# Adding the last block's rows of a routed expert layer from SBUF with one-hot products instead of through memory

## The reference, cut to what matters

```python
vl = rmsnorm(hl, norm2_g[i]) * (1.0 + sc2) + sh2
hl = hl + g2 * moe_ffn(vl, ...)          # i = 0, then Hyena, then i = 1
...
def moe_ffn(xt, ...):
    # best group of 4, two best experts of its 8, weights g_w * e_w
    ...                                   # rows sorted by expert into blocks
    gate, up = split(xblk @ w13[e], 2)
    yb = (silu(gate) * up) @ w2[e]
    return segment_sum(yb * row_w[:, None], row_tok)
...
return rmsnorm(hl, final_g)
```

## Time and profile before

| What | Value |
|---|---|
| Runs | 2173.26 us median (2172.42 to 2173.95) |
| The profiled execution's own time | 2173.9 us |
| Its span | 2172.2 us, 21060 instructions |
| Mean granted TensorE clock | 0.977 of full |
| PE busy | 2006.0 us (92%) |
| DVE, ACT, POOL busy | 798.1, 399.3, 237.8 us (37%, 18%, 11%) |
| DMA | 582.54 MB, mean 268 GB/s |
| Copy of the hidden values (line 856), once per block | 73 times |
| Scatters (line 478) | 73 |

### The profile page before, as it was taken

One profiled execution on the slowest core, in us unless ns is written; L12 is line 12 of the kernel. 1 busy time (PEld: TensorE's weight loads), 2 busy tenths in 40 slices (PEclk: granted clock), 3 DMA queues, 4 the chain that ended last, 5 costly groups with the idle time before them and its releaser, 6 DMA issues. The chain is left out here.

```text
span 2172.2 us, 21060 instructions
## 1 busy us (share of the span) xinstructions
PE 2006.0 (92%) x7704; PEld 894.5 (41%) x7704; DVE 798.1 (37%) x1599; ACT 399.3 (18%) x813; POOL 237.8 (11%) x517
## 2 busy tenths in 40 slices
PE   5999999999999979999999988999997999888883
PEld 2555444454444544433333334444554344333331
DVE  3777321245323252225223524474735122111113
ACT  2111213223200121132113212110002111111111
POOL 1000000000000012212222210000000222222221
PEclk9999999999999979999999999999998999999997
DMA  9899432231114289999999973120255999999995
GB/s 369 300 372 355 167 124 90 90 109 61 58 59 148 88 357 407 392 411 420 414 422 400 422 277 119 62 91 26 103 246 205 392 421 421 423 422 422 422 422 218
DMA packets 117567, 582.54 MB, mean 268 GB/s; under 512 B 25599, under 2 KB 43255, under 8 KB 78028
## 3 DMA queue, kind: packets, MB, share of 16 engines
q1 hardware_dynamic: 90892, 538.32, 62.0%
q10 hardware_dynamic: 14560, 26.12, 3.4%
q0 software_dynamic: 12000, 16.62, 2.1%
HBM read 565.62 MB, written 38.12 MB: 278 GB/s over the span
## 5 line engine op out<-in xcount | busy, mean ns | idle before, releaser
L628 PE MATMUL bank<-w,xT 128*64 128x512 f32 x1856 | 414.0, 593 | 17.4 <-DMA w<-in_moe_w 16.3
L648 PE MATMUL bank<-w,hT 128*64 128x512 f32 x1168 | 273.3, 610 | 31.8 <-DMA w<-in_moe_w 23.7
L628 PEld LDWEIGHTS bank<-w,xT 128*64 128x64 f32 x1856 | 145.6, 137 | 271.9 <-issue 251.1
L856 DVE COPY hT<-bank 128x256 f32<-128x256 f32 x73 | 31.0, 424 | 451.8 <-PE bank L636 451.8
L1290 PE MATMUL bank<-uhi,wnh 128*128 128x512 f32 x384 | 168.4, 593 | 0.9 <-ACT uhi L1047 0.9
L648 PEld LDWEIGHTS bank<-w,hT 128*64 128x64 f32 x1168 | 87.0, 139 | 179.1 <-issue 151.7
L540 ACT ACTIVATE oh<-bank 128x256 f32<-128x256 f32 x73 | 28.0, 384 | 698.3 <-PE bank L628 698.3
L1688 PE MATMUL bank<-uT,wo 128*128 128x512 f32 x256 | 133.1, 602 | 3.0 <-DMA wo<-in_m_in_w 3.0
L861 DVE TENSOR_TENSOR ohs<-bank,g2h 128x512 f32<-128x512 f32 x73 | 50.5, 692 | 209.2 <-PE bank L648 209.2
L628 PE MATMUL bank<-w13x,xT 128*64 128x512 f32 x480 | 109.1, 594 | 4.0 <-DMA w13x<-in_moe_w 4.0
L1290 PEld LDWEIGHTS bank<-uhi,wnh 128*128 128x128 f32 x384 | 71.8, 190 | 86.9 <-issue 85.8
(11 more groups left out here) (453 smaller groups left out, 2237.2 us busy)
## 6 DMA issues: line engine op xcount, KB each, us to landing
w<-in_moe_w SPq DMA_DIRECT2D x172, 2048.0 KB, 19.4
adab<-in_ada_w SPq DMA_DIRECT2D x24, 2048.0 KB, 11.5
w13x<-in_moe_w SPq DMA_DIRECT2D x23, 2048.0 KB, 16.7
wnh<-in_h_in_w SPq DMA_DIRECT2D x12, 1024.0 KB, 5.2
wo<-in_m_in_w SPq DMA_DIRECT2D x4, 2048.0 KB, 17.8
wo<-in_m_in_w ACTq DMA_DIRECT2D x4, 2048.0 KB, 21.6
ow<-in_m_out_w SPq DMA_DIRECT2D x8, 1024.0 KB, 7.5
d_xm<-xmb ACTq DMA_DIRECT2D x16, 385.5 KB, 7.5
```

The lines of the kernel that those rows point to most:

```text
L628: ins = t_.matmul(b[n * C:(n + 1) * C, :].rearrange("c (g f) -> c g f", g=2), xT[:, k, half * C:(half + 1) * C], w13s[i][:, k, n], start=( ...
L648: ins = t_.matmul(b_y[m * C:(m + 1) * C, :], hT[:, k, half * C:(half + 1) * C], w2[:, u, kk, m * 512:(m + 1) * 512], start=(kk == 0), stop ...
```

## The change

The rows of block 36 (the last of the 36 steps) are no longer scattered. From the routing DVE builds, at step 3, a matrix over tokens and rows that holds the routing weight where a token's choice lies in block 36 (`last_hot`); at step 4 PE turns it (`last_turn`) and DVE copies it to `lastT`. In `drain`, PE multiplies it with `yb` (`last_rows`: eight products of 64 rows by 512 columns, into eight banks), and DVE adds the eight banks to `hl`. PE's first `extra` waits for all eight adds. Because some rows of `d_y` are now never written, `blank_results` fills each `d_y` with zeros beforehand: in `c4` for layer 0, in the Hyena stage for layer 1.

`load_results` moves from the start of the next stage to the end of SP's work in the expert stage, behind a new semaphore `end` that POOL raises when its scatters have landed. It now has fixed buffers in the weight rings. The router tables of layer 1 are loaded from ACT's queue late in the Hyena stage. `one32` becomes a slice of `ones`; `ohb` shares memory with `lastT`, and the new one-hot tiles lie in `dfe`. Cut to its core:

```diff
+LAST_TURN = 4
...
+        results = [[put(f"yg{l}{i}", [P, 4, D], W13 + pos * HALF) for i, pos in enumerate(((3, 4), (0, 1))[l])] for l in range(2)]
+        yg = [[tile_[:, 2 * i:2 * i + 2, :] for tile_ in results[l] for i in range(2)] for l in range(2)]
...
+        def blank_results(sp, l, blank, s_):
+            sp.dma_start(d_y[l].rearrange("(p a) (b n) -> p (a b) n", p=P, b=2), blank[:].to_broadcast([P, 16, 512])).then_inc(s_, 16)
...
+                LASTB = (0, 1, 2, 3, 6, 7, 4, 5)
+                def scattered(n):
+                    return len([b for b in range(1, n + 1) if b % 2 == n % 2 and b != NS])
...
@@ expert stage, SP
                     steps(sp, main, lambda: None, extra)
-                    if l == 0:
-                        load_route_tables(sp, 1)
+                    sp.wait_ge(S["end"], 1)
+                    load_results(sp, l)
@@ expert stage, POOL
                     def drain():
-                        scatter(NS)
                         for s in range(NS, NS + NB):
...
                     for u in range(2):
-                        pool.wait_ge(s_yst[u], (NS + u) // 2 * 16)
+                        pool.wait_ge(s_yst[u], 16 * scattered(NS - 1 + (NS - 1 + u) % 2))
+                    g.tensor_tensor(pad[:, 2 * NB:], ident[:, 0:2], ident[:, 0:2], ALU.add).then_inc(S["end"], 1)
@@ expert stage, PE, in main(s), before product2(s)
+                        if s == LAST_TURN:
+                            last_turn()
...
+                    def last_turn():
+                        pe.wait_ge(S["oh"], 1)
+                        for t in range(TL):
+                            ins = t_.transpose(bank[7][:, t * P:(t + 1) * P], ohl[:, t, :], ident[:])
+                        ins.then_inc(S["ohT"], 1)
+                    def last_rows():
+                        pe.wait_ge(S["ya"], NS)
+                        pe.wait_ge(S["xTa"], NS)
+                        pe.wait_ge(S["xTv"], NS)
+                        for t in range(TL):
+                            for m in range(2):
+                                rows = slice(m * C, (m + 1) * C)
+                                t_.matmul(bank[LASTB[2 * t + m]][:], lastT[rows, t * P:(t + 1) * P], yb[NS % 2][rows, :], start=True, stop=True).then_inc(S["lr"], 1)
                     def drain():
                         h_transposes(NS)
                         product2(NS)
+                        last_rows()
                     def extra(s):
+                        pe.wait_ge(S["la"], 2 * TL)
                         first(s)
@@ expert stage, DVE, at the end of main(b)
+                        if b == LAST_TURN - 1:
+                            last_hot()
+                        if b == LAST_TURN:
+                            dve.wait_ge(S["ohT"], 1)
+                            own(v.tensor_copy(lastT[:], bank[7][:]))
+                    def last_hot():
+                        own(v.tensor_scalar(sbf[:], sbf[:], float(NS - 1), 2.0 * P, ALU.not_equal, ALU.mult))
+                        own(v.tensor_tensor(spf[:], spf[:], sbf[:], ALU.add))
+                        own(v.tensor_tensor(eq, i64[:].to_broadcast([P, 2 * TL, P]), spf[:].to_broadcast([P, 2 * TL, P]), ALU.is_equal))
+                        pairs = eq.rearrange("p (t k) n -> p t k n", k=2)
+                        own(v.tensor_tensor(pairs, pairs, wts[:].rearrange("p k (t o) -> p t k o", o=1).to_broadcast([P, TL, 2, P]), ALU.mult))
+                        v.tensor_tensor(ohl, pairs[:, :, 0], pairs[:, :, 1], ALU.add).then_inc(S["oh"], 1)
...
                     def drain():
                         h_turned(NS)
                         y_out(NS)
+                        for i in range(2 * TL):
+                            rows = hl[:, i // 2, i % 2 * 512:(i % 2 + 1) * 512]
+                            dve.wait_ge(S["lr"], i + 1)
+                            v.tensor_tensor(rows, rows, bank[LASTB[i]][:], ALU.add).then_inc(S["la"], 1)
@@ Hyena stage, SP
-                    load_results(sp, 0, yg, s_yg)
...
                         load_slab(sp, wn, s_wn, q)
+                        if q == 4:
+                            sp.wait_ge(S["pad"], 3)
+                            blank_results(sp, 1, blank, S["yz"])
@@ Hyena stage, ACT, before the squares for the router
+                    load_route_tables(act, 1)
@@ c4, SP
                 load_w13(sp, 0, 2)
+                sp.wait_ge(s_blank, 1)
+                blank_results(sp, 0, blank, s_yz)
                 sp.wait_ge(s_o4, TL)
@@ final stage, SP
-                load_results(sp, 1, yg, s_yg)
```

More of the change, by code:

```diff
@@ L183, in build @@
         s_rt = [sem(f"s_rt{l}") for l in range(2)]
+        s_yg = [[sem(f"s_yg{k}{t}") for t in range(TL)] for k in range(2)]
+        results = [[put(f"yg{l}{i}", [P, 4, D], W13 + pos * HALF) for i, pos in enumerate(((3, 4), (0, 1))[l])] for l in range(2)]
+        yg = [[tile_[:, 2 * i:2 * i + 2, :] for tile_ in results[l] for i in range(2)] for l in range(2)]
         def route_tables():
@@ L269, in load_w2, with load_results, add_results @@
             sp.dma_start(w2t[l][:, u].rearrange("p (h k) n -> p h k n", h=2), w2_view(l)[:, u]).then_inc(s_w2[l][u], 16)
[L271 removed]
+        def blank_results(sp, l, blank, s_):
+            sp.dma_start(d_y[l].rearrange("(p a) (b n) -> p (a b) n", p=P, b=2), blank[:].to_broadcast([P, 16, 512])).then_inc(s_, 16)
+        def load_results(sp, l):
             for t in range(TL):
                 for k in range(2):
[L274 to L276 removed]
+                    sp.dma_start(yg[l][t][:, k, :], d_y[l].rearrange("(t p k) d -> t k p d", p=P, k=2)[t, k]).then_inc(s_yg[k][t], 16)
+        def add_results(dve, own, l, t):
             for k in range(2):
[L278 to L279 removed]
+                dve.wait_ge(s_yg[k][t], 16 * (l + 1))
+                own(nc.vector.scalar_tensor_tensor(out=hl[:, t, :], in0=yg[l][t][:, k, :], scalar=wts[:, k, t:t + 1], in1=hl[:, t, :], op0=ALU.mult, op1=ALU.add))
         def expert_ffn(l):
@@ L770, in _ @@
                     own(v.tensor_scalar(isd[:], key[:], m8[:, PAIRS - 1:PAIRS], None, ALU.is_ge))
-                    own(v.tensor_tensor_scan(out=idx[:], data0=one32[:], data1=isd[:], initial=0.0, op0=ALU.mult, op1=ALU.add))
+                    own(v.tensor_tensor_scan(out=idx[:], data0=one32, data1=isd[:], initial=0.0, op0=ALU.mult, op1=ALU.add))
                     own(v.tensor_tensor(idx[:], er, idx[:], ALU.subtract))
@@ L800, in _ @@
                     own(v.tensor_scalar(nov[:], nov[:], 0.0, None, ALU.max))
-                    own(v.tensor_tensor_scan(out=ovr, data0=one32[:], data1=nov[:], initial=0.0, op0=ALU.mult, op1=ALU.add))
+                    own(v.tensor_tensor_scan(out=ovr, data0=one32, data1=nov[:], initial=0.0, op0=ALU.mult, op1=ALU.add))
                     own(v.tensor_tensor(der, ovr, nov[:], ALU.subtract))
@@ L858, in y_out @@
                     def y_out(n):
-                        at_least(dve, s_yst[n % 2], (n - 1) // 2 * 16)
+                        at_least(dve, s_yst[n % 2], 16 * (scattered(n) - (n != NS)))
                         dve.wait_ge(S["yp"], n)
@@ L1019, in _ @@
                     load_w13(sp, 1, 2)
+                    sp.wait_ge(S["yz"], 16)
                 @blk.gpsimd
@@ L1097, in _ @@
                     for t in range(TL):
-                        add_results(dve, own, t, yg, s_yg)
+                        add_results(dve, own, 0, t)
                         v.memset(r1[:, t:t + 1], 0.0).then_inc(S["hl"], 1)
@@ L2288, in _ @@
                 load_w13(sp, 0, 1)
+                sp.wait_ge(s_yz, 16)
+            @blk.gpsimd
+            def _(pool):
+                nc.gpsimd.memset(blank[:], 0.0).then_inc(s_blank, 1)
             @blk.scalar
@@ L2446, in _ @@
                 for t in range(TL):
-                    add_results(dve, own, t, yg, s_yg)
+                    add_results(dve, own, 1, t)
                     v.memset(r1[:, t:t + 1], 0.0).then_inc(s_hlf, 1)
```

36 lines of the change are left out of this document (17 added, 19 removed).

## The result

The changed kernel took **2185.16 us** (median of six runs, 2183.49 to 2189.78) beside 2174.54 for the kernel before: a ratio of 1.0044, interval 1.0031 to 1.0058, so 10.6 us slower. The forecast was 2183.4, with a range of 2178 to 2188. The profiled execution took 2184.7 around a span of 2183.0.

What follows compares the result with a forecast made beforehand. PE was the busiest engine, its largest wait 23.7 us for expert weights; the change touches the two expert stages' ends. Layer 0 +11.9 and layer 1 -1.8 make +10.1 on the 2173.3 median: 2183.4 us, range 2178 to 2188.

Steps and rivals of the forecast that it cites:

- The stall at the overflow block: Layer 0: PE's overflow block waits for eight products and eight DVE adds, resuming at 1280.85, not 1273.45; +7.4 us.
- Rival 1: Last block's eight products don't overlap, 0.43 us a record; 1.5 us more at each end, 2186.4; chance 0.09.
- rival 5: Overflow block's first product would have been held up anyway, so the 7.4 us vanish; chance 0.10.
- Eight issues before the boundary: End of layer 0: SP issues eight fetches before the boundary while every engine waits, with POOL's instruction; +4.5 us.
- Early adds worth 0: Hyena stage's start: adds begin about 4.1 us earlier, costed at nothing because PE's spectra and ACT set the same time.
- Rival 4: Adds alone gate the Hyena stage, so the 4.1 us come back; 2179.3; chance 0.08.
- Layer 1, -1.8: End of layer 1, no overflow block: final adds end at 2157.9 in place of 2159.70, without the wait in the middle.
- rival 2: PE idles some 2.6 us before the overflow block, whose product then runs at the lower clock; +2.5, 2185.9; chance 0.08.
- (d): Zeros into the result arrays, projection and Hyena stages: 4.19 MB each, some 10 us, hidden where the DMA engines idle.
- (a) to (c): Expert stages, under cover: building one-hot rows on DVE (3.8 us), four PE transposes (0.65), a DVE copy (0.69).
- (f): Late Hyena stage: layer 1's router tables on ACT's queue beside the output weights; taken as 0, at most 4 us.
- rival 3: Router tables delay the output weights in the Hyena stage; up to +4, 2187.4; chance 0.05.

Runs made afterwards that it cites:

- e1: Changed kernel, but layer 0 scatters its block 36 again, without one-hot rows, products and their wait; median 2.5 us over the kernel before.
- e2: Changed kernel, but layer 0's results are fetched at the start of the Hyena stage as before; median 4.1 us over the kernel before.
- e4: Changed kernel with ScalarE's copies of the second odd spectrum behind the fourth square; first spectrum to layer 1's first scatter 399.7 us, changed kernel 402.9.
- e5: Kernel before with ScalarE's copies of the second odd spectrum moved behind the fourth square; norm scale still 17.74 us behind the Hyena stage's first spectrum.
- b0: Changed kernel with layer 0's scatter and Hyena-stage fetches restored, fetches split over two queues, ScalarE's spectrum copies behind the fourth square; 1.0 us below the kernel before.
- e3: Changed kernel with layer 0 scattering and fetching as before, layer 1, blanks and tables as changed; 2172.4 us, 4.1 below the kernel before.
- e8: Changed kernel with every blank written twice, second to an unread array; first spectrum to layer 1's first scatter 402.9 us, as in the changed kernel.
- a_again: The changed kernel measured once more, nothing altered; median 2189.9 us, profiled span 2189.2, which is 6.2 longer than in the first measurement.

## Why the prediction was right, point by point

- *The stall at the overflow block, +7.4.* Measured 7.13, and gone in e1. The mechanism held in detail: products at 0.23 a record, adds every 0.60. Rival 1 (no overlap, 0.43 a record) fell with it, and rival 5 (the overflow block has cover) with e1.
- *Eight issues before the boundary, +4.5.* The two profiles gave 3.56, e2 gave 4.9 by the rows behind `end`, and all traces of such fetches 4.6 to 5.6. The mechanism was right and the size a little low; what blurred it was the scatter's landing.
- *Early adds worth 0.* C stayed at 17.74, and e2 took them away without a loss. Its reason, ScalarE's wait for TensorE, is shown by e4: with the wait out of the way 3.7 us appear. Rival 4 fell. The prediction had named both chains to the norm scale, and e5 and b0 show the other one: there the norm scale comes 2.5 us behind the end of the last add.
- *Layer 1, -1.8.* Measured -1.7, and e3 has it alone. The boundary took 1.70, not 1.4; the adds began 0.2 earlier than the terms said.
- *The clock, rival 2.* TensorE ran at a granted 1.00 (2.4 GHz) before and behind the idle 2.38 us, where 4.79 us of idling had brought 0.50, so rival 2 fell:

```profile
1282.00:1286.00 4.00, 3.77 (x18) 1.35 (x20) 0.18 (x1) 0.00 (x0) 0.00 (x0) 1.00 0.00 0
```

- *Cover.* (d) held, with a second blank besides (e8). (a) to (c) and (e) had no run of their own. From the first scatter to block 36's second product the changed kernel took 0.8 us more in layer 0 and 0.3 in layer 1. In layer 0 this says nothing: traces with the same code there lie between 453.4 and 455.7 us. In layer 1 it does not look like chance: the twelve traces with the one-hot rows took 438.6 to 439.0 us, the two without them 438.2 and 438.3. So some 0.5 us of (a) to (c) probably lies open there, which the prediction put at nothing.
- *(f), rival 3.* No cost, as forecast, but for another reason. The 4 us at most were a bound on what the output weights lose. They lost nothing; the tables did, 37 to 46 us for three of them, and 19.35 us of VectorE's wait took most of a cover that I had not costed. TensorE's first row transpose came 14.8 us behind the tables' use (1637.36 - 1622.56).
- *The sum, +10.1.* By rows 7.1 + 3.6 - 1.7 = 9.0, by spans 10.8, by medians 10.6. The remainder of 1.8 lies before the first scatter of layer 0 (0.9) and in blocks 1 to 36 of the two layers (0.8 and 0.3), less 0.2 elsewhere; it is smaller than the 6.2 that a_again shows for one kernel. That 10.1 and 10.6 agree so closely is in part luck: the early scatter of the changed profile took off about a microsecond, this remainder put more than that back, and a second measurement gave 14.5. What is shown is the terms.

## What to carry to other kernels

Moving rows from memory to SBUF removes a scatter only where the scatter is waited for: in the layer with an overflow block it was covered, and its replacement stood ahead of the next product. A fetch put ahead of a barrier costs its issues there, so it has to shorten what ends last behind the barrier; look for a second chain of the same length before counting the gain. And a load cut into many small packets beside a full stream on another queue advances by about one packet for each of the stream's; here three of the four small tables took 37 to 46 us by it.

## What the runs showed that I had not expected

- Two queues shared the DMA engines packet for packet, 574 to 572 in 20 us, though the packets differed in size (14.5 KB and 120 bytes).
- The scatter of 256 KB landed in 3.0 us in some executions and in 3.7 to 4.1 in others of nearly the same code.
- Issuing eight fetches from two queues halved the issue time (2.2 in place of 4.2 to 5.2 us), but the first rows came 0.8 later.
- The first spectrum of the Hyena stage, 16 records behind 6 to 12 us of idling, took 8.5 to 9.9 us; this alone moves everything behind it by over a microsecond between executions.
- The profiled span of one kernel varied by 6.2 us, with a granted clock of 0.977 and 0.975 as means.
